# The first high part on VectorE, one more warm-up matmul, squares between the last pieces, the fourth unit ahead of the root's table, the last reciprocal ahead of a wait

## The chip, the cores and the metric

The kernel runs on one core of one Trainium2 chip. The metric is the device time of one execution in microseconds (us), the median of three runs. All input is in the chip's memory (HBM) at the start, and the output is written back there.

## What is computed

Two transformer blocks, one after the other, on a sequence of 256 tokens of width 1024, all in fp32. Cut to the steps:

```
# block 1
h = rmsnorm(x); proj = h @ w_in                  # 1024 -> 3*256 + 3*512 + 3*256
y = [stick_breaking_attention | chunked_relpos_attention | short_conv_mixer]
x = x + group_rmsnorm(y) @ w_out
x = x + (silu(n @ w_gate) * (n @ w_up)) @ w_down  # n = rmsnorm(x), width 2816
# block 2
h = rms_norm(x); proj = h @ w_in_2               # z_a, q, k, v, gate logits
y_a = chunked_spatial_gating(gelu(z_a)); y_b = dilated_mixture_attention(q, k, v)
x = x + (gate0 * (y_a @ w_branch_a) + gate1 * (y_b @ w_branch_b)) @ w_out_2
x = x + (gelu(conv3(a)) * val) @ w_down_2         # [a, val] = rms_norm(x) @ w_up_2
return rms_norm(x, final_norm_g)
```

rmsnorm(x, w) is x * rsqrt(mean(x*x) + 1e-6) * w. The change touches the first rmsnorm with the first units of the first product, and the last rms_norm.

## The kernel before

**Units.** All weights are laid out as one stream of units, each 128 partitions x 2048 columns of fp32 (1 MB). A ring of three slots holds them (RING = 3). SyncE's queue loads unit u into `raw[u % 3]` once the low part of unit u-3 is made (semaphore `unit_lo`). ScalarE casts the unit to fp32r, the high part (`split`, L525, writes `whi`, counts `unit_hi`), and VectorE subtracts it from the original, the low part (`split`, L978, writes `wlo`, counts `unit_lo`). TensorE multiplies high x high, low x high and high x low (helper `three`, L1594 to L1596; in other stages `tiles`, L1601 and L1602), which gives nearly fp32 accuracy at the speed of fp32r. The activations are split in the same way: `h_high` on ScalarE (L533) and `h_low` on VectorE (L989). Each engine runs its own instructions strictly in the order of the program; the order between engines comes from semaphores alone.

**The start.** The first three units come in ten pieces (`PIECES`): four of 512 columns for unit 0, four for unit 1, two of 1024 for unit 2. The activations x arrive transposed in five chunks. For each k of 8 ScalarE does `h_high(k)` and `split_piece(k)` (L530), VectorE `h_low(k)` and `split_piece(k)` (L984). TensorE first does WARM_UP = 8 matmuls of ones by ones (L1942), whose result nobody reads, and then `first_unit(0)` and `first_unit(1)`: for each k two matmuls of high x high (L1641), two with the low part of the weights (L1644), two with the low part of the activations (L1647). Behind the ten pieces ScalarE squares x in four steps (`square2`, L540), computes a small gain, and loads the table of the square root (`root_table`, L537). VectorE adds the squares (`fold(0)`, L995 to L998). Units 2 and 3 are `pair_unit`s: 24 matmuls for one half of the tokens, then 24 for the other half, and between the halves of unit 2 the sum of squares over the partitions (`stats(0)`, L1799).

**Behind it.** A hand-written order follows, the same on each engine: for n = 1, 2, ... a `split` of unit n + 2, then what the attention needs at that point. ScalarE at n = 2 issues the load of the bias table `relb` on its own queue (L677), takes the root (`root(0)`, L546), and scales q into `qkv_b` (L552); at n = 3 it casts unit 5 and squares q (`b_square(0)`, L630). VectorE sums these squares (`b_sums`, L1081) and normalises q (`b_norm`, L1087 and L1089). Between the halves of unit 4 TensorE transposes it (`turn_b(0)`, L1590).

**The end.** The last matmuls give the second half of the columns for tokens 128 to 255. VectorE adds them to x (L1576), multiplies by the gain (`final_gained`, L1549) and waits for this product (semaphore `dve_order`); ScalarE squares and takes the root (L958 to L960, L946); VectorE forms the reciprocal (L1563, in `final_scale`) and scales 640 columns (L1566), ScalarE the other 384 (L949), and six transfers in all write the output. `done` is a helper that lets the engine wait for its own instruction.

Of the kernel before, what the change touches and what calls it, by code (L numbers as in the profile page):

```python
# [33 lines left out]
HALF = UNIT // 2  # L34
UF = 256
WIDE = 512
WARM_UP = 8
RING = 3

D_SB, D_CH, D_CV = 256, 512, 256  # L40
# [190 lines left out]
def build(nc, A, out):  # L231
    with ExitStack() as ctx:
# [3 lines left out]
        def sem(name):  # L236
            return ctx.enter_context(nc.semaphore(name))
# [84 lines left out]
        bank = [psum[:, b, :] for b in range(8)]  # L322

        piece_loaded = [sem(f"piece_loaded{q}") for q in range(len(PIECES))]
        piece_hi, piece_lo = sem("piece_hi"), sem("piece_lo")
        unit_loaded = [sem(f"unit_loaded{s}") for s in range(RING)]
        unit_hi, unit_lo, unit_used = sem("unit_hi"), sem("unit_lo"), sem("unit_used")
        psum_full = [sem(f"psum_full{b}") for b in range(8)]
# [179 lines left out]
        def _(act):  # L508
# [18 lines left out]
            def split_piece(q):  # L527
                u, a, b = PIECES[q]
                act.wait_ge(unit_loaded[u % RING] if b == UNIT else piece_loaded[q], 16)
                act.copy(whi[u % RING][:, a:b], raw[u % RING][:, a:b]).then_inc(unit_hi if b == UNIT else piece_hi, 1)  # L530
# [8 lines left out]
            def square2(b):  # L539
                act.activation(sq[:, 2 * b:2 * b + 2, :], x[:, 2 * b:2 * b + 2, :], ACT.Square).then_inc(squares, 1)  # L540

            def root(n):

                b = STATS_BANK[n]
                full(act, b, ("stats", n))
                act.activation(rb[:], bank[b][:, 0:T], ACT.Sqrt, bias=EPS, scale=1.0 / D).then_inc(psum_free[b], 1)  # L546
# [41 lines left out]
            for k in range(KT):  # L588
                act.wait_ge(x_loaded[next(c for c, (a, b) in enumerate(X_CHUNKS) if a <= k < b)], 16)
                h_high("attn_norm", k)  # L590
                split_piece(k)
            split_piece(8)
            split_piece(9)
            for b in range(4):
                square2(b)
            act.wait_ge(cols_loaded, 16)
            act.activation(qgain[:], col("q_norm"), ACT.Copy, scale=HD ** -0.5).then_inc(act_order, 1)
            n_order[0] += 1
# [71 lines left out]
                return qkv_b[:, t, c:c + D_CH]  # L670

            for n in range(1, len(IN1)):
                if n == 1:
                    split(3)
                if n == 2:
                    split(4)
                    act.dma_start(relb[:], A["relb"]).then_inc(bias_loaded, 16)  # L677
                    root(0)
                    act.wait_ge(r_ready, 1)
                    evac_tokens(1, "qb", 0, qkv_cols("qb", 0))  # L680
                    evac_tokens(1, "qb", 1, qkv_cols("qb", 1))
                if n == 3:
                    split(5)
                    for t in range(TT):
                        freed(act, 6 + t, ("in1", "qb"))
                    b_square(0)
                    evac_tokens(1, "kb", 0, qkv_cols("kb", 0))
                    b_root(0)
                if n == 4:
                    evac_tokens(1, "kb", 1, qkv_cols("kb", 1))  # L690
                    for t in range(TT):
                        freed(act, t, ("in1", "kb"))
                    b_square(1)
                    split(6)
                    b_gains(0)
                    b_root(1)
                if n == 5:
                    split(7)
                    b_gains(1)
                    evac_tokens(1, "vb", 0, qkv_cols("vb", 0))  # L700
                if n == 6:
                    evac_tokens(1, "vb", 1, qkv_cols("vb", 1))
                    split(8)
                    b_exp(0)
                    b_exp(1)
                if n == 7:
                    b_evac_pt(0)
                    b_evac_pt(1)
                    split(9)
                    b_exp(2)  # L710
                    b_exp(3)
                if n == 8:
                    b_evac_pt(2)
                    b_evac_pt(3)
                    split(10)
                    b_exp(4)
                    b_exp(5)
                    for h in range(H_SB):
                        freed(act, ZA[h], ("za", h))
                    done(act.activation(E[:], Z[:], ACT.Abs))  # L720
                    done(act.activation(E[:], E[:], ACT.Exp, scale=-1.0))
                if n == 9:
                    full(act, 0, ("in1", "va"))
                    for t in range(TT):
                        ins = act.activation(v_a[:, t, :], bank[0][:, t * UF:(t + 1) * UF], ACT.Copy, scale=rcol[:, t:t + 1])
                    ins.then_inc(psum_free[0], 1)
                    b_evac_pt(4)
                    b_evac_pt(5)
                    split(11)
                    b_exp(6)  # L730
                    b_exp(7)
                    act.activation(E[:], E[:], ACT.Ln, bias=1.0).then_inc(z_soft, 1)
                if n == 10:
                    y_square(0)
                    b_evac_pt(6)
                    b_evac_pt(7)
                    split(U_OUT1)
                    y_rms(0)
                if n == 11:
                    split(U_OUT1 + 1)  # L740
                    freed(act, 0, ("in1", "xc"))
                    for f in range(2):
                        act.activation(cv[:, f, :], hc[:, f, 2:T + 2], ACT.Copy, scale=col("conv1", 3 * f + 2))\
                           .then_inc(cv_tap, 1)
                    y_square(1)
                    y_rms(1)
                    y_high(0)
                    for h in range(H_SB):
                        freed(act, AA[h], ("aa", h))
                    act.activation(E[:], Z[:], ACT.Exp).then_inc(z_w, 1)  # L750
# [213 lines left out]
        def _(dve):  # L964
# [15 lines left out]
            def split_piece(q):  # L980
                u, a, b = PIECES[q]
                s = u % RING
                dve.wait_ge(*((unit_hi, u + 1) if b == UNIT else (piece_hi, pieces_before(u) + 1 + a // (b - a))))
                dve.tensor_tensor(wlo[s][:, a:b], raw[s][:, a:b], whi[s][:, a:b], ALU.subtract)\  # L984
                   .then_inc(unit_lo if b == UNIT else piece_lo, 1)

# [2 lines left out]
                dve.scalar_tensor_tensor(lo[:, k, :], x[:, k, :], col(gain, k), hi[:, k, :], ALU.mult, ALU.subtract)\  # L989
                   .then_inc(h_lo, 1)  # L990

            def fold(n):

                dve.wait_ge(squares, 4 * n + 2)
                done(dve.tensor_tensor(sq[:, 0:2, :], sq[:, 0:2, :], sq[:, 2:4, :], ALU.add))  # L995
                dve.wait_ge(squares, 4 * n + 4)
                done(dve.tensor_tensor(sq[:, 4:6, :], sq[:, 4:6, :], sq[:, 6:8, :], ALU.add))
                ins = dve.tensor_tensor(sq[:, 0:2, :], sq[:, 0:2, :], sq[:, 4:6, :], ALU.add)  # L998
                if n == 0:
                    ins.then_inc(folded, 1)  # L1000
                else:
                    done(ins)
                    dve.tensor_tensor(sq[:, 0, :], sq[:, 0, :], sq[:, 1, :], ALU.add).then_inc(folded, 1)

            def gather(squares0, f):

# [61 lines left out]
                return dve.tensor_tensor(dst, dst, bc(rb[:], 1, 2), ALU.mult)  # L1068

            dve.wait_ge(consts, 1)  # L1070
            for k in range(KT):
                h_low("attn_norm", 0, k)
                split_piece(k)
            split_piece(8)
            split_piece(9)
            fold(0)

            def b_sums(j):

# [115 lines left out]
            def log_weights(h):  # L1195

                full(dve, AA[h], ("aa", h))
                dve.tensor_tensor(Z[:, h, :], Z[:, h, :], bank[AA[h]][:, 0:3 * P], ALU.add).then_inc(psum_free[AA[h]], 1)

            for n in range(1, len(IN1)):  # L1200
                if n == 1:
                    split(3)
                if n == 2:
                    rms_columns(0)
                    split(4)
# [73 lines left out]
                    h_low("ffn_norm", 1, 2 * b - 2)  # L1279
                    h_low("ffn_norm", 1, 2 * b - 1)  # L1280
            split(U_FF1 + 1)
            fold(1)

            def masks2():

# [265 lines left out]
            for u in range(U_DOWN2, N_UNITS):  # L1551
                split(u + 2)
                if u == U_DOWN2 + 6:
# [5 lines left out]
                    dve.wait_ge(final_sq, 2)  # L1559
                    dve.tensor_scalar(root_in, ss[:, 0:2], 1.0 / D, EPS, ALU.mult, ALU.add).then_inc(final_part, 1)  # L1560
            def final_scale(t):
                dve.wait_ge(final_root, t + 1)
                dve.reciprocal(root_out[:, t:t + 1], root_out[:, t:t + 1]).then_inc(final_r, 1)  # L1563
                dve.wait_ge(final_r, t + 1)
                for c in (slice(0, DVE_OUT // 2), slice(DVE_OUT // 2, DVE_OUT)):
                    dve.tensor_scalar(xg[:, t, c], xg[:, t, c], root_out[:, t:t + 1], None, ALU.mult).then_inc(out_ready, 1)  # L1566

            final_add(2)
            done(final_gained(2))
            final_scale(0)  # L1570
            final_add(3)
            for b, a, w in ((1, 0, CUT), (0, CUT, WIDE - CUT)):
# [7 lines left out]
               .then_inc(final_part, 1)  # L1580
            for b in range(2):
                freed(dve, b, ("rest2", b))
            done(final_gained(3))
            final_scale(1)


        @block.tensor
        def _(pe):
# [43 lines left out]
            def first_unit(u):  # L1632


                for kk in range(KT // 2):
                    k, w, last = u * KT // 2 + kk, slice(kk * WIDE, (kk + 1) * WIDE), kk == KT // 2 - 1
                    tokens = [slice(t * P, (t + 1) * P) for t in range(TT)]
                    pe.wait_ge(h_hi, k + 1)
                    pe.wait_ge(*((unit_hi, u + 1) if last else (piece_hi, pieces_before(u) + 1 + kk)))
                    for t, c in enumerate(tokens):  # L1640
                        pe.matmul(bank[6 + t][:], hh[:, k, c], whi[u][:, w], start=k == 0, stop=False)  # L1641
                    pe.wait_ge(*((unit_lo, u + 1) if last else (piece_lo, pieces_before(u) + 1 + kk)))
# [589 lines left out]
```

## Time and profile before

| | |
|---|---|
| median of 3 runs | 695.69 us (695.29 to 696.03) |
| the profiled execution | 695.99 us, of which the span is 694.0 us |
| TensorE matmul busy | 685.1 us, 99% of the span |
| VectorE busy | 498.4 us, 72% |
| ScalarE busy | 401.6 us, 58% |
| GpSimd busy | 9.4 us, 1% |
| read from HBM | 122.36 MB, 178 GB/s over the span |

The span is the time from the first to the last instruction of the core; the execution has 2.0 us more around it. Times in the rows are counted from the span's start. PE is TensorE, DVE VectorE, ACT ScalarE, SP SyncE; a letter q behind the engine means its queue. A row of the timeline gives start, duration, engine, line, operation, output<-inputs, shapes, and in brackets the idle time ahead of it with what ended it. Each instruction's record holds some pipeline time at its end, so that records of one engine overlap by 0.1 to 0.2 us: the distance from start to start is what an instruction costs in a row of them.

### The profile page before, as it was taken

Reading aid. Unit: us, or ns where it says so; the run is one execution under the profiler, and the core shown is the slowest. Engines: PE = TensorE matmul, PEld = TensorE weight load, DVE = VectorE, ACT = ScalarE, POOL = GpSimd, SP = SyncE. Lnnn points to the kernel's source line nnn. Section 1 sums busy time; section 2 is a strip of 40 time slices with the busy share of each in tenths; the row PEclk is TensorE's granted clock in tenths of the full one; section 3 lists DMA queues with packets and bytes.
Section 4 is the critical chain, followed back from the end, with each engine's and each line's share of the span. In section 5 each row is a group of like instructions: output and inputs, shape, how many; then the busy total and the mean of one; then the engine's idle time right before and its main releaser. Section 6 shows DMA issues by size and latency. Waiting matters only on the chain.

```text
span 694.0 us, 10061 instructions
## 1 busy us (share of the span) xinstructions
PE 685.1 (99%) x4118; PEld 602.7 (87%) x4118; DVE 498.4 (72%) x689; ACT 401.6 (58%) x504; POOL 9.4 (1%) x25
## 2 busy tenths in 40 slices
PE   8999999999999999999999999999999999999996
PEld 7889999888888888888878888899978888888885
DVE  5866677979986766666565477687779988886353
ACT  6875866755555554464457565564557666664342
POOL 1000000003000000000000000000000000000000
PEclk9999999999999999999999999999999999999999
DMA  8863225655565555545435346454555655554511
GB/s 322 316 232 135 90 93 183 220 183 193 179 219 187 194 182 182 187 178 193 171 124 180 122 138 226 160 181 146 182 211 182 203 184 189 200 196 175 190 60 61
DMA packets 19773, 124.05 MB, mean 179 GB/s; under 512 B 2320, under 2 KB 3472, under 8 KB 5520
## 3 DMA queue, kind: packets, MB, share of 16 engines
q1 hardware_dynamic: 18432, 120.07, 48.8%
q10 hardware_dynamic: 1296, 3.35, 1.4%
q8 instruction: 32, 0.52, 0.3%
q14 instruction: 13, 0.11, 0.0%
HBM read 122.36 MB, written 1.05 MB: 178 GB/s over the span
## 4 chain that ended last, share of the span: by engine, by line
PE 90%; DVE 4%; ACT 3%; issue 1%; DMA 1%; DVEq 0%; ACTq 0%
PE psum L1601 34%; PE psum L1602 18%; PE psum L1594 10%; PE psum L1596 10%; PE psum L1595 10%; PE psum L1590 2%; DVE wlo L978 2%; ACT whi L525 2%; PE psum L1641 1%; PE psum L2073 1%; PE psum L1647 1%; PE psum L1644 1%; DMA x<-in_xT 1%; PE psum L2121 0%; DVE gates L1496 0%
## 5 line engine op out<-in xcount | busy, mean ns | idle before, releaser
L978 DVE TENSOR_TENSOR wlo<-raw,whi 128x2048 fp32r<-128x2048 f32 x110 | 251.7, 2290 | 78.2 <-ACT whi L525 78.1
L525 ACT CAST whi<-raw 128x2048 fp32r<-128x2048 f32 x110 | 209.7, 1908 | 44.7 <-PE psum L1596 38.4
L1601 PE MATMUL psum<-hx,whi 128*128 128x512 f32 x528 | 183.6, 391 | 0.0
L1602 PE MATMUL psum<-hx,wlo 128*128 128x256 f32 x528 | 148.9, 282 | 0.0
L1601 PE MATMUL psum<-yx,whi 128*128 128x512 f32 x352 | 123.3, 393 | 1.1 <-DVE yx L989 1.0
L1601 PEld LDWEIGHTS psum<-hx,whi 128*128 128x128 f32 x528 | 99.1, 188 | 20.9 <-issue 0.2
L1602 PEld LDWEIGHTS psum<-hx,wlo 128*128 128x128 f32 x528 | 99.8, 189 | 0.0
L1602 PE MATMUL psum<-yx,wlo 128*128 128x256 f32 x352 | 99.2, 282 | 0.0
L1601 PEld LDWEIGHTS psum<-yx,whi 128*128 128x128 f32 x352 | 66.0, 188 | 15.7 <-DVE yx L989 2.1
L1602 PEld LDWEIGHTS psum<-yx,wlo 128*128 128x128 f32 x352 | 66.5, 189 | 0.0
L1601 PE MATMUL psum<-G,whi 128*128 128x512 f32 x176 | 61.8, 393 | 0.0
L1594 PE MATMUL psum<-whi,hx 128*128 128x512 f32 (+1 forms) x144 | 56.5, 392 | 0.0
L1595 PE MATMUL psum<-wlo,hx 128*128 128x512 f32 (+1 forms) x144 | 55.1, 383 | 0.0
L1596 PE MATMUL psum<-whi,hx 128*128 128x512 f32 (+1 forms) x144 | 55.1, 383 | 0.0
L1602 PE MATMUL psum<-G,wlo 128*128 128x256 f32 x176 | 49.8, 283 | 0.0
L1594 PE MATMUL psum<-hx,whi 128*128 128x256 f32 x144 | 41.0, 285 | 0.2 <-DVE hx L1509 0.2
L1595 PE MATMUL psum<-hx,whi 128*128 128x256 f32 x144 | 40.3, 280 | 0.0
L1596 PE MATMUL psum<-hx,wlo 128*128 128x256 f32 x144 | 40.2, 279 | 0.0
L1601 PEld LDWEIGHTS psum<-G,whi 128*128 128x128 f32 x176 | 33.1, 188 | 7.6
L807 ACT COPY us<-psum 128x512 f32<-128x512 f32 x22 | 12.9, 585 | 42.4 <-PE psum L1602 42.4
L800 ACT COPY side<-psum 128x512 f32<-128x512 f32 x22 | 12.9, 585 | 40.0 <-PE psum L1602 40.0
L1594 PE MATMUL psum<-yx,whi 128*128 128x256 f32 x128 | 36.0, 281 | 0.0
(271 smaller groups left out, 1107.0 us busy)
## 6 DMA issues: line engine op xcount, KB each, us to landing
raw<-in_stream SPq DMA_DIRECT2D x110, 1024.0 KB, 4.7
raw<-in_stream SPq DMA_DIRECT2D x8, 256.0 KB, 5.5
relb<-in_relb ACTq DMA_DIRECT2D x1, 1536.0 KB, 9.7
raw<-in_stream SPq DMA_DIRECT2D x2, 512.0 KB, 7.7
x<-in_xT SPq DMA_DIRECT2D x3, 256.0 KB, 5.5
out_t<-sq SPq DMA_DIRECT2D x4, 160.0 KB, 2.4
final_gain<-in_final_gain ACTq DMA_DIRECT2D x1, 512.0 KB, 3.5
bsp<-in_bsp ACTq DMA_DIRECT2D x1, 384.0 KB, 3.4
```

The costliest lines, as they stand in the source:

```text
L525: act.copy(whi[s][:], raw[s][:]).then_inc(unit_hi, 1)
L800: act.copy(side[:], psum[:, 0:2, T:2 * T]).then_inc(gate_side, 1)
L807: act.copy(us[:], psum[:, 2:4, T:2 * T]).then_inc(up_side, 1)
L978: dve.tensor_tensor(wlo[s][:], raw[s][:], whi[s][:], ALU.subtract).then_inc(unit_lo, 1)
L1590: return pe.transpose(out_, in_, ident[:])
L1594: pe.matmul(dst, stat[0], mov[0], start=first, stop=False, **kw)
L1595: pe.matmul(dst, stat[0], mov[1], start=False, stop=False, **kw)
L1596: return pe.matmul(dst, stat[1], mov[0], start=False, stop=last, **kw)
L1601: pe.matmul(bank[b][:], stat[0], mov, start=first, stop=False, skip_group_check=True)
L1602: return pe.matmul(bank[b][:, 0:T], stat[1], mov[:, 0, :], start=False, stop=last, skip_group_check=True)
L1641: pe.matmul(bank[6 + t][:], hh[:, k, c], whi[u][:, w], start=k == 0, stop=False)
L1644: pe.matmul(bank[6 + t][:], hh[:, k, c], wlo[u][:, w], start=False, stop=False)
```

## The change

Five edits:

1. VectorE, not ScalarE, makes the high part of piece 0, with a copy, and signals it on a new semaphore `first_hi`. VectorE and TensorE wait for it there; the counts on `piece_hi` are one lower in all other places.
2. WARM_UP is 9 instead of 8.
3. ScalarE squares x between the last pieces, and VectorE adds each pair of squares as it comes (`first_fold`, three adds in a chain) instead of `fold(0)`. The second block's fold keeps its form under the name `second_fold`.
4. ScalarE casts unit 3 right behind the squares, ahead of the small gain and the root's table; at n = 2 the load of the bias table and the root come ahead of the cast of unit 4. VectorE's order of its subtractions is as before.
5. In `final_scale` the product with the gain is issued, then the reciprocal waits only for the root, and the wait for the product stands behind the reciprocal.

```diff
-WARM_UP = 8
+WARM_UP = 9
@@ ScalarE
             for k in range(KT):
                 act.wait_ge(x_loaded[...], 16)
                 h_high("attn_norm", k)
-                split_piece(k)
+                if k:
+                    split_piece(k)
+            square2(0)
             split_piece(8)
+            square2(1)
             split_piece(9)
-            for b in range(4):
-                square2(b)
+            square2(2)
+            square2(3)
+            split(3)
             act.wait_ge(cols_loaded, 16)
@@
             for n in range(1, len(IN1)):
-                if n == 1:
-                    split(3)
                 if n == 2:
-                    split(4)
                     act.dma_start(relb[:], A["relb"]).then_inc(bias_loaded, 16)
                     root(0)
+                    split(4)
                     act.wait_ge(r_ready, 1)
@@ VectorE
             def split_piece(q):
                 u, a, b = PIECES[q]
                 s = u % RING
-                dve.wait_ge(*((unit_hi, u + 1) if b == UNIT else (piece_hi, pieces_before(u) + 1 + a // (b - a))))
+                if q == 0:
+                    dve.wait_ge(first_hi, 1)
+                elif b == UNIT:
+                    dve.wait_ge(unit_hi, u + 1)
+                else:
+                    dve.wait_ge(piece_hi, pieces_before(u) + a // (b - a))
@@
+            def first_fold(b):
+
+                dve.wait_ge(squares, b + 1)
+                if b > 1:
+                    dve.wait_ge(dve_order, n_order[0])
+                ins = dve.tensor_tensor(sq[:, 0:2, :], sq[:, 0:2, :], sq[:, 2 * b:2 * b + 2, :], ALU.add)
+                if b == 3:
+                    ins.then_inc(folded, 1)
+                else:
+                    ins.then_inc(dve_order, 1)
+                    n_order[0] += 1
@@
             dve.wait_ge(consts, 1)
-            for k in range(KT):
+
+            dve.wait_ge(piece_loaded[0], 16)
+            dve.tensor_copy(whi[0][:, 0:WIDE], raw[0][:, 0:WIDE]).then_inc(first_hi, 1)
+            split_piece(0)
+            h_low("attn_norm", 0, 0)
+            for k in range(1, KT):
                 h_low("attn_norm", 0, k)
                 split_piece(k)
             split_piece(8)
+            first_fold(1)
             split_piece(9)
-            fold(0)
+            first_fold(2)
+            first_fold(3)
@@
             def final_scale(t):
+                final_gained(2 + t).then_inc(dve_order, 1)
+                n_order[0] += 1
                 dve.wait_ge(final_root, t + 1)
                 dve.reciprocal(root_out[:, t:t + 1], root_out[:, t:t + 1]).then_inc(final_r, 1)
+                dve.wait_ge(dve_order, n_order[0])
                 dve.wait_ge(final_r, t + 1)
@@
-            done(final_gained(2))
             final_scale(0)
@@
-            done(final_gained(3))
             final_scale(1)
@@ TensorE
                     pe.wait_ge(h_hi, k + 1)
-                    pe.wait_ge(*((unit_hi, u + 1) if last else (piece_hi, pieces_before(u) + 1 + kk)))
+                    if k == 0:
+                        pe.wait_ge(first_hi, 1)
+                    else:
+                        pe.wait_ge(*((unit_hi, u + 1) if last else (piece_hi, pieces_before(u) + kk)))
```

## Rows read from the trace of the kernel before

**Rows 1.** Parts 1 and 2 of the page: busy time; TensorE's granted clock

```profile
PE 685.1 (99%) x4118; PEld 602.7 (87%) x4118; DVE 498.4 (72%) x689; ACT 401.6 (58%) x504; POOL 9.4 (1%) x25
...
PEclk9999999999999999999999999999999999999999
```

**Rows 2.** TensorE's waits, whole span: total us, times, longest

```profile
PE psum L1641 <- ACT whi L530: 0.7, 1, 0.7
```

**Rows 3.** Chain in order of time, first 12 us: start, duration

```profile
4.38 0.51 ACT hx L533
...
5.54 1.19 PE psum L1641 x2
...
8.44 0.84 PE psum L1641 x2
9.28 0.46 PE psum L1644 x2
```

**Rows 4.** Timelines of TensorE and VectorE, first 10 us

```profile
1.07 3.78 PE L1942 MATMUL psum<-ones 128*128 128x128 f32 x16 [1.07 <-POOL ones L469]
...
6.86 0.69 DVE L984 TENSOR_TENSOR wlo<-raw,whi 128x512 fp32r<-128x512 f32 x1 [0.34 <-ACT whi L530]
...
8.49 0.69 DVE L984 TENSOR_TENSOR wlo<-raw,whi 128x512 fp32r<-128x512 f32 x1 [0.55 <-ACT whi L530]
```

**Rows 5.** Transfers issued at 0.8 us: KB, us from issue to landing

```profile
raw<-in_stream SPq DMA_DIRECT2D x1, 256.0 KB, 3.4
```

**Rows 6.** Groups of VectorE by form: busy us, mean ns

```profile
L1290 DVE TENSOR_SCALAR mask<-mask 128x384 f32<-128x384 f32 x3 | 1.1, 362 | 0.1
```

**Rows 7.** Timelines of ScalarE, VectorE and TensorE, 15 to 24 us

```profile
15.70 1.06 ACT L530 CAST whi<-raw 128x1024 fp32r<-128x1024 f32 x1 [0.20 <-DMA raw<-in_stream]
...
20.37 3.91 ACT L525 CAST whi<-raw 128x2048 fp32r<-128x2048 f32 x2
...
19.68 0.69 DVE L998 TENSOR_TENSOR sq<-sq 128x512 f32<-128x512 f32 x1
...
18.44 0.40 PE L1594 MATMUL psum<-whi,hx 128*128 128x512 f32 x1
...
21.23 1.02 PE L1799 MATMUL psum<-sq,ones 128*128 128x256 f32 x4
```

**Rows 8.** Timelines of ScalarE, VectorE and TensorE, 26 to 34 us

```profile
26.61 1.91 ACT L525 CAST whi<-raw 128x2048 fp32r<-128x2048 f32 x1
28.41 1.06 ACT L630 ACTIVATE Z<-qkv_b 128x1024 f32<-128x1024 f32 x1
...
29.76 1.22 DVE L1081 TENSOR_REDUCE small<-Z 128x16 f32<-128x1024 f32 x1
...
31.55 1.22 DVE L1089 TENSOR_TENSOR qkv_b<-qkv_b,small 128x1024 f32<-128x1024 f32 x1
...
33.29 1.03 PE L1590 MATMUL psum<-ident,qkv_b 128*128 128x128 f32 x8
```

**Rows 9.** Transfers issued at 10.2, 18.0 and 22.4 us: KB, us to landing

```profile
raw<-in_stream SPq DMA_DIRECT2D x1, 1024.0 KB, 7.9
...
raw<-in_stream SPq DMA_DIRECT2D x1, 1024.0 KB, 8.3
...
relb<-in_relb ACTq DMA_DIRECT2D x1, 1536.0 KB, 9.7
```

**Rows 10.** Timelines of ScalarE and VectorE, 683 to 690 us

```profile
689.09 0.29 ACT L946 ACTIVATE small<-small 128x1 f32<-128x1 f32 x1
...
688.59 0.69 DVE L1549 TENSOR_TENSOR sq<-xt,final_gain 128x512 f32<-128x512 f32 x1
689.83 0.16 DVE L1563 RECIPROCAL small<-small 128x1 f32<-128x1 f32 x1 [0.55 <-ACT small L946]
...
683.62 0.29 ACT L946 ACTIVATE small<-small 128x1 f32<-128x1 f32 x1
...
684.02 0.17 DVE L1563 RECIPROCAL small<-small 128x1 f32<-128x1 f32 x1 [0.52 <-ACT small L946]
```

More of the change, by code:

```diff
@@ L324, in build @@
         piece_loaded = [sem(f"piece_loaded{q}") for q in range(len(PIECES))]
-        piece_hi, piece_lo = sem("piece_hi"), sem("piece_lo")
+        first_hi, piece_hi, piece_lo = sem("first_hi"), sem("piece_hi"), sem("piece_lo")
         unit_loaded = [sem(f"unit_loaded{s}") for s in range(RING)]
@@ L990, in h_low, with second_fold @@
                    .then_inc(h_lo, 1)
[L992 to L999, printed above, removed]
+            def first_fold(b):
[4 more added lines that the diff above has]
+                if b == 3:
                     ins.then_inc(folded, 1)
                 else:
-                    done(ins)
-                    dve.tensor_tensor(sq[:, 0, :], sq[:, 0, :], sq[:, 1, :], ALU.add).then_inc(folded, 1)
+                    ins.then_inc(dve_order, 1)
+                    n_order[0] += 1
+            def second_fold():
+                dve.wait_ge(squares, 6)
+                done(dve.tensor_tensor(sq[:, 0:2, :], sq[:, 0:2, :], sq[:, 2:4, :], ALU.add))
+                dve.wait_ge(squares, 8)
+                done(dve.tensor_tensor(sq[:, 4:6, :], sq[:, 4:6, :], sq[:, 6:8, :], ALU.add))
+                done(dve.tensor_tensor(sq[:, 0:2, :], sq[:, 0:2, :], sq[:, 4:6, :], ALU.add))
+                dve.tensor_tensor(sq[:, 0, :], sq[:, 0, :], sq[:, 1, :], ALU.add).then_inc(folded, 1)
             def gather(squares0, f):
@@ L1198, in log_weights @@
                 dve.tensor_tensor(Z[:, h, :], Z[:, h, :], bank[AA[h]][:, 0:3 * P], ALU.add).then_inc(psum_free[AA[h]], 1)
+            split(3)
             for n in range(1, len(IN1)):
-                if n == 1:
-                    split(3)
                 if n == 2:
@@ L1281, in _ @@
             split(U_FF1 + 1)
-            fold(1)
+            second_fold()
             def masks2():
```

## Prediction

> **What bounds the kernel now.** I read the page first: TensorE is busy for 685.1 of 694.0 us [rows 1]. Only what is left, some 9 us, can be had without taking work away. Next the view of TensorE's waits: 0.7 us lie before the first real matmul [rows 2], and the other waits are those of the start-up and some 1 us in the second block, far behind anything that is edited here. From the last matmul to the end of the span another 5.8 us pass, in which VectorE, ScalarE and the output transfers work. So a change at the front pays if TensorE's stream starts earlier or runs faster there, and if nothing behind it is then late; one at the tail pays in full.
>
> The chain of waits over the first 10 us shows two things [rows 3]. The stream is held by ScalarE, which does both halves of the first step in turn, the scaled activation at 4.38 and the first weight piece at 4.89; the first pair of matmuls starts at 5.54. And a pair of 512-column matmuls takes 0.84 us up to 9.28 and 0.46 us afterwards: TensorE runs at the lower of its two levels (1.2 GHz) until then, at 2.4 GHz from then on (the granted clock of the page reads 9 of 10 throughout, so the rows of the matmuls decide). Before the rise TensorE did eight warm-up matmuls from 1.07 to 4.85, sat idle for 0.69 us, and then worked without a gap [rows 2, 4].
>
> **The first high part on VectorE.** The first piece of weights lands 3.4 us after its issue at 0.81, at 4.2 [rows 5], before ScalarE begins its activation. VectorE has nothing to do until that activation ends at 4.89, since its first operation reads it. The copy of 128x512 has no row of its own: a one-source operation over 128x384 takes 0.36 us, the two-source one over 128x512 takes 0.69 [rows 4, 6]. So it ends between 4.7 and 4.95; I take 4.8, nearer the one-source row. ScalarE's activation ends at 4.89 [rows 3] and is the later of the two in most cases. Adding 0.14 from the end to the first matmul, as in the chain, the stream starts at 5.1, some 0.45 us earlier. At the low clock this is worth half, 0.23 us, if the clock still rises at 9.3. VectorE's low part is then due by 6.0 and is done by 5.6 at worst (4.95 and one 0.69): no new wait.
>
> The Trainium skill ("VectorE: DVE Perf Modes", mode 2x_2P) says that a copy from SBUF of 32-bit data can run at two elements a cycle, which two-source operations can't. The 0.36 against 0.69 us agrees; with 0.43 us the copy would be hidden behind ScalarE, with 0.69 it would decide, and the sum would differ by 0.03 us.
>
> **One more warm-up.** Eight took 3.78 us, 0.43 to 0.47 each [rows 4]. The ninth ends near 5.3 in the records; matmul records overlap by about 0.2 us, so its successor can start at 5.1. It costs nothing beyond the start found above and closes the idle 0.69 us. What that does to the clock no row shows. Lower bound: nothing, rise at 9.3. Upper bound: the rise comes at once, near the first real matmul. I take the early rise, because the only thing that TensorE lacked in its first 4.8 us against the stretch before 9.28 is that gap. TensorE can then run only as fast as the pieces come: the second piece's low part ends at 6.86+0.69=7.55, the third's at 8.49+0.69=9.18 [rows 4]; both hang on transfers, which the change leaves alone. With the third low part matmul pairs start at 9.3; from there two pairs (0.93 us) finish this step and five more steps of three pairs (1.40 us) follow: 9.3+0.93+7.0=17.25. Unit 2 begins at 18.44 now [rows 7]. Gain at this point: 1.2 us.
>
> The skill ("TensorE: Matmul & The Clock Gate", the HAM clock gate) says that sustained activity releases the clock, and also that the moment is not tied to the kernel's start and varies between runs. By the first half the early rise is likely; by the second no one profile can promise it, and the spread of 0.74 us among the three runs shown would in part be this.
>
> **Squares between the last pieces, and the fold in three adds.** ScalarE waits for both of the 1024-column pieces to land, 0.20 us for the second [rows 7], and half a us of square goes ahead of each, which these waits take up in part; the second piece's cast moves from 15.70 to 15.95. VectorE's second low part then ends at 18.5 instead of 18.0, just when a TensorE that is 1.2 us ahead wants it (17.25+1.4=18.65). The old fold ends at 20.37 and TensorE's sum of squares begins at 21.23 [rows 7]; 1.2 us earlier that would be 20.0, a 0.3 us wait. The new fold ends at about 19.9. So this edit is worth nothing alone and covers 0.3 us of the gain.
>
> **The fourth unit ahead of the root's table.** The table load goes behind the cast, which starts at 20.37 now [rows 7]; it can start at about 18.15, when the unit lands (10.2+7.9) [rows 9], 2.2 us earlier, and VectorE's low part with it: 18.15+1.9+2.3=22.4. TensorE takes that unit at about 21.23+0.9+2.8=24.9 now (the sum of squares, then twelve steps as from 18.44 to 21.23), at 23.7 if it is 1.2 ahead. Again cover, no gain by itself. The swap has more in it: the transfer of the bias table (1.5 MB, ScalarE's queue) is issued at about 21.6 instead of 22.4 [rows 9], the root comes before the fifth unit's cast, and SyncE's queue issues unit 5 at 18.55 instead of 18.05, as it waits for the second piece's low part, and unit 6 at 22.4, 2.2 us earlier.
>
> **What is late next.** Halfway through unit 4 TensorE transposes the normalised q (start 33.29). Its input is VectorE's multiply, which ends at 31.55+1.22=32.77 [rows 8]. With 0.13 us from there to TensorE, the slack is 0.38 us, less than the gain of 1.2. The chain behind it: unit 5, issued at 18.05, lands 8.3 us later at 26.35 [rows 9], ScalarE casts it at 26.61, then squares q at 28.41, VectorE sums at 29.76, and 3.01 us later the multiply is done [rows 8]. Now VectorE's long reciprocal also ends just before 29.76; after the change its work is some 1 us earlier, so the landing L of unit 5 decides: squares L+1.80, sums L+2.89, ready L+5.90, transposes L+6.03. With L as now 32.38, a gain of 0.91. L can move: unit 5's last bytes already share the engines with the bias table (9.7 us for 1.5 MB), which now starts 0.8 us earlier. I take L=26.5, gain 0.75; bounds 0.3 (L 0.6 later) and the full 1.2. Later transposes have more than 1 us of slack, and from unit 6 on everything is paced by TensorE.
>
> **The tail.** In the last chain ScalarE's root ends at 689.39, yet VectorE's reciprocal starts at 689.83, 0.44 us later, and its own multiply ended at 689.28; for the other tokens the root ended at 683.91 and the reciprocal began at 684.02 [rows 10]. The reciprocal is the instruction that carries the wait for VectorE's own multiply; the change moves this wait behind it. If the 0.4 us belong to the wait, ScalarE's part of the output gains 0.4 (VectorE's less, as its scaling now carries the wait); if not, one wait less is about 0.05. I take 0.25. A loss is excluded: the multiply is still issued before the root is there.
>
> **The sum.** Profiled execution 695.99 us (span 694.0 and 2.0 around it), less 0.75 and 0.25, is 695.0. The median of the runs shown is 0.3 us lower; the same 1.0 us from it gives 694.7.
>
> **The rivals.**
> 1. The gap was not what held the clock. The rise stays at 9.3, the front gives 0.23, nothing behind is late. 0.23+0.25=0.5 us: 695.2 (694.9 to 695.6). For it: the warm-ups are 128-column fp32 matmuls, not the later kind. Against it: nothing else differs before the rise. The same time comes out if the copy on VectorE is late.
> 2. Slower: the bias table, 0.8 us earlier, holds up unit 5's last bytes. Place: ScalarE's cast of unit 5, ahead of the square of q. It decides from L=27.25, where the transposes start as late as now. At L=28 TensorE loses 0.7 us, less 0.25 at the tail: 696.1. Against it: unit 5's bulk is in before the table starts.
> 3. Slower: the rise moves later, since it is not tied to the start. Each us later costs half a us, 3 us later 1.5, less the 0.5 of rival 1: 696.7.
> 4. More: unit 5 lands by 26.0, all 1.2 us pass, the tail gives 0.4, and the runs of before had the rise on average later than the profiled one (each us half a us): 693.8.
>
> **How the numbers follow.** Forecast 0.55 (694.1 to 695.3, from gains of 1.6 and 0.35), rival 1 0.25, rival 2 0.05, rival 3 0.05, rival 4 0.10. The range leaves out rivals 2 and 3 and the far end of 4: 693.9 to 695.6. A measurement of this kernel can tell some 0.2% (1.4 us) from no change, so faster means below 694.3: rival 4 and somewhat over a third of the forecast's case, 0.32. Slower means above 697.1: only rival 3 with a yet later rise, 0.05. The rest, 0.63, is the same.
>
> **What would show it.** Early rise: pairs of 0.46 us before 8 us and waits for the second and third piece. Cap at the transposes: TensorE waits up to 0.9 us for VectorE's multiply near 32.5. Rival 1: pairs of 0.84 us until about 9, no wait at all after the first. Rival 2: unit 5's cast after 27. Tail: reciprocal within 0.1 us of the root. The prediction is wrong if the transposes do not wait although the clock rose early, or if a step outside the first 35 us and the last 6 moves.

## The result and the profile after

The changed kernel takes 698.02 us (median of 12 runs, 695.82 to 700.37) against 695.35 (12 runs, 694.74 to 696.46): ratio 1.0031, 95% interval 1.0017 to 1.0046. It is slower by 0.3%, where 1.0 us of gain was forecast. The profiled execution took 696.45 us with a span of 694.7, against 694.0 before.

The start went as forecast. TensorE's timeline (start, duration; answers to [rows 4] and to the chain of [rows 3]):

```profile
1.07 4.21 PE L1967 MATMUL psum<-ones 128*128 128x128 f32 x18 [1.07 <-POOL ones L469]
4.99 0.97 PE L1666 MATMUL psum<-whi,hx 128*128 128x512 f32 x2
5.81 0.63 PE L1669 MATMUL psum<-wlo,hx 128*128 128x512 f32 x2
6.27 0.63 PE L1672 MATMUL psum<-whi,hx 128*128 128x512 f32 x2
```

No idle time stands ahead of the first real matmul any more, it starts at 4.99, and the pair that starts at 5.81 takes 0.46 us: the pace is that of the upper clock level, 3.5 us earlier than in the profile of before. (The granted clock reads 1.00 in both profiles all through the first 10 us, so, as in the prediction, it is the pace of the matmuls that decides. The pairs up to 9.8 us are further apart by up to 0.2 us, as TensorE now waits for the second and the third piece.) The copy on VectorE took 0.43 us and was over ahead of ScalarE's activation.

The loss is at the transposes of the normalised q. TensorE's waits, first 60 us, and its timeline around 32 us (answers to [rows 2] and [rows 8]):

```profile
PE psum L1612 <- DVE qkv_b L1111: 2.0, 1, 2.0
```

```profile
31.90 0.40 PE L1618 MATMUL psum<-whi,hx 128*128 128x512 f32 x1
34.30 1.09 PE L1612 MATMUL psum<-ident,qkv_b 128*128 128x128 f32 x8 [2.00 <-DVE qkv_b L1111]
```

TensorE comes to the transposes at 31.90+0.23=32.13, 1.16 us earlier than before, and can start them only at 34.30, 1.01 us later than before. ScalarE's timeline says where it comes from (answers to [rows 7] to [rows 9]; the last two are the views of the transfers issued at 17.9 on ScalarE's queue and at 18.2 on SyncE's, KB and us to landing):

```profile
17.84 1.91 ACT L525 CAST whi<-raw 128x2048 fp32r<-128x2048 f32 x1 [0.18 <-DMA raw<-in_stream]
17.85 0.33 ACTq L678 DMA_DIRECT2D relb<-in_relb  x1
19.66 0.20 ACT L601 ACTIVATE qgain<-cols 128x1 f32<-128x1 f32 x1
19.87 1.28 ACT L537 ACT_TABLE_LOAD   x1
...
28.27 1.91 ACT L525 CAST whi<-raw 128x2048 fp32r<-128x2048 f32 x1 [3.66 <-DMA raw<-in_stream]
```

```profile
relb<-in_relb ACTq DMA_DIRECT2D x1, 1536.0 KB, 9.2
...
raw<-in_stream SPq DMA_DIRECT2D x1, 1024.0 KB, 10.1
```

The load of the bias table stands in the program behind the cast of unit 3, the small gain and the root's table, which are over at 21.4. It was issued at 17.85, in the moment in which the cast of unit 3 began: here the computing ahead of a transfer did not hold its issue back, only the waits ahead of it did (here the last to be met is that for unit 3's landing). So it went out 0.3 us ahead of unit 5 (issued at 18.16) and 4.5 us earlier than before. The queues in 19.5 to 21.5 us (packets, MB, share of the 16 engines), changed kernel:

```profile
q10 hardware_dynamic: 59, 0.72, 89.4%
q1 hardware_dynamic: 5, 0.01, 1.1%
```

q10 is ScalarE's queue, q1 SyncE's: the bias table moves, unit 5 does not. Unit 5 lands at 28.3, ScalarE waits 3.66 us for it.

The tail gained. VectorE and ScalarE (answers to [rows 10]):

```profile
690.17 0.29 ACT L948 ACTIVATE small<-small 128x1 f32<-128x1 f32 x1
...
690.49 0.16 DVE L1586 RECIPROCAL small<-small 128x1 f32<-128x1 f32 x1
690.76 0.68 DVE L1590 TENSOR_SCALAR sq<-sq,small 128x320 f32<-128x320 f32 x2
```

The reciprocal starts 0.03 us behind the root's end instead of 0.44. From VectorE's last addition (689.29, before 688.21) to the span's end it is 5.4 us, before 5.8: 0.38 us less. The 1.08 us by which that addition is later and the 0.38 us back give the 0.7 us by which the profiled spans differ.

That leaves some 1.6 us between this profile and the median. Each run has its span and its mean granted TensorE clock. Five of the twelve, the profiled one among them, have spans of 694.1 to 694.9 us at 0.998 or 0.999; seven have 696.2 to 698.6 at 0.995 or 0.996. The 33 runs of before that stand beside the first experiments lie at 0.997 to 0.999. So in over half of the runs of the changed kernel the clock was low somewhere for longer; where, no profile of this kernel shows, as none was taken of such a run.

### The profile page after: what moved, and what is told of

Its sections match the earlier page's. It is cut to its first block, busy times and chain, and to the rows that moved or that the text cites. A ratio compares the mean times of both kernels' runs of the same rounds, so it can differ in the third digit from the quotient of the medians.

```text
span 694.7 us, 10066 instructions
## 1 busy us (share of the span) xinstructions
PE 684.7 (99%) x4120; PEld 601.5 (87%) x4120; DVE 498.9 (72%) x690; ACT 400.8 (58%) x503; POOL 9.3 (1%) x25
## 4 chain that ended last, share of the span: by engine, by line
PE 86%; DVE 5%; ACT 4%; DMA 2%; issue 2%; SPq 1%; DVEq 0%; ACTq 0%
PE psum L1623 34%; PE psum L1624 18%; PE psum L1616 10%; PE psum L1617 9%; PE psum L1618 9%; DMA raw<-in_stream 2%; PE psum L1612 2%; DVE wlo L980 2%; ACT whi L525 2%; PE psum L2098 1%; PE psum L2146 0%; DVE gates L1517 0%; SPq L428 0%; PE psum L2086 0%; DVE wlo L991 0%
```

## The experiments

The theories when they began. A: the bias table goes ahead of unit 5, TensorE idles 2 us at the transposes, and that idle time makes the clock fall in some of the runs. B: the clock falls because a TensorE that is fast from 5.6 us on has to wait for pieces in the first 10 us. C: the squares between the pieces and ScalarE's new order make the normalised q late. Each kernel has 10 to 12 runs, one has 7; each ratio is against the kernel before on the same chip.

**The bias table behind unit 5.** The changed kernel with

```diff
                 if n == 2:
-                    act.dma_start(relb[:], A["relb"]).then_inc(bias_loaded, 16)
                     root(0)
                     split(4)
...
                 if n == 3:
                     split(5)
+                    act.dma_start(relb[:], A["relb"]).then_inc(bias_loaded, 16)
```

> The changed kernel, with one line moved: the load of the bias table is issued behind ScalarE's cast of unit 5 (whose wait holds the issue back until unit 5 has landed) instead of ahead of the root. Theory A (the table's 1.5 MB, issued at 17.85, go ahead of unit 5; TensorE then waits 2.0 us for the normalised q, and in about half of the runs the clock falls because of that gap): unit 5 lands by 26.3, the transposes start by 32.4, TensorE's wait is under 0.5 us, all runs within 1 us of each other, clock 0.998 or more in all, median about 694.0 us. Theory B (the clock falls because TensorE, fast from 5.6 us on, waits for the second to third piece in the first 10 us): the spread of several us and clocks of 0.995 stay in about half of the runs, median 696 or more. Theory C (the squares between the pieces and the new order of ScalarE are late): unit 5 is cast early but the wait at the transposes stays near 2 us.

Measured: 694.17 us (693.83 to 694.51), ratio 0.9979 (0.9970 to 0.9988), the clock 0.997 to 0.999 in all eleven runs. ScalarE's and TensorE's timelines:

```profile
24.16 1.91 ACT L525 CAST whi<-raw 128x2048 fp32r<-128x2048 f32 x1
24.17 0.34 ACTq L685 DMA_DIRECT2D relb<-in_relb  x1
```

```profile
31.88 1.03 PE L1612 MATMUL psum<-ident,qkv_b 128*128 128x128 f32 x8
```

The queues in 19.5 to 21.5 us, to be set beside those above:

```profile
q1 hardware_dynamic: 96, 0.77, 95.7%
```

Unit 5 has landed when ScalarE wants it, the transposes start at 31.88 with no wait, 1.41 us earlier than before the change, and with the tail's 0.38 the span is 1.8 us shorter (692.2). One line turns the 0.3% loss into a 0.2% gain; this kernel (from here on the mended kernel) beats both. B and C are out: the early rise and the new order are all still in it, and the next kernel's profile has the waits for pieces in the first 10 us too.

**Behind unit 4.**

```diff
-                    act.dma_start(relb[:], A["relb"]).then_inc(bias_loaded, 16)
                     root(0)
                     split(4)
+                    act.dma_start(relb[:], A["relb"]).then_inc(bias_loaded, 16)
```

> The changed kernel, with the load of the bias table issued behind ScalarE's cast of unit 4, so at the landing of unit 4 (20.3 in the changed kernel's trace) instead of 17.85. Theory A: the table shares the engines with unit 5 for part of its way; unit 5 lands between 26 and 27.5, the transposes start between 32.1 and 33.6, median 694.3 to 695.5 us, a low clock only where the wait comes near 1.5 us, so rarely. Theory B: as slow and as spread as the changed kernel. Theory C: wait as in the changed kernel, 2 us.

Measured: 694.16 us (693.89 to 694.85), ratio 0.9981 (0.9972 to 0.9990). The table was issued at 20.80. Unit 4 had landed at 20.0 already; the last wait ahead of the issue is here the root's, for TensorE's sum of squares, whose last record ends at 20.69. Unit 5, issued at 17.95, landed 5.1 us later, earlier than theory A had it. Three us of delay for the table are as good as six: most of unit 5 has moved before the table's bytes begin.

**The bias table early, and nothing else.** The kernel before with

```diff
                 if n == 1:
                     split(3)
+                    act.dma_start(relb[:], A["relb"]).then_inc(bias_loaded, 16)
                 if n == 2:
                     split(4)
-                    act.dma_start(relb[:], A["relb"]).then_inc(bias_loaded, 16)
```

> The kernel before, with the load of the bias table issued behind the cast of unit 3 (about 20.4 us) instead of behind that of unit 4 (22.4). Nothing of the start is changed, so the clock rises as before and TensorE never waits in the first 10 us. Theory A: unit 5 lands some 1 to 2 us later, 27.3 to 28.3, the transposes start at 33.4 to 34.4 instead of 33.3, median 0.1 to 1.0 us above the kernel before, with single runs 1.5 us longer and at a clock of 0.995 if the wait is long enough. Theories B and C: as the kernel before, 695.4 us.

Measured: 696.58 us (695.11 to 698.68), ratio 1.0016 (1.0006 to 1.0026). The issue did not come at 20.4, as I had expected even then, but at 17.57, while ScalarE still had the root's table to load:

```profile
17.57 0.33 ACTq L675 DMA_DIRECT2D relb<-in_relb  x1
19.75 3.70 ACT L525 CAST whi<-raw 128x2048 fp32r<-128x2048 f32 x2
27.93 1.90 ACT L525 CAST whi<-raw 128x2048 fp32r<-128x2048 f32 x1 [1.91 <-DMA raw<-in_stream]
```

The transposes start at 33.96, after a wait of 1.3 us. The loss can be made from the kernel before by this one line. Unit 5 was issued 0.13 us ahead of the table here (17.44) and landed late all the same, at 27.9: from 20.0 to 22.5 us it moved 0.46 MB and the table 0.59. So the table does not have to overtake unit 5, to run beside it is enough. A run of 698.68 us has a clock of 0.996; the other ten have 0.997 to 0.999. The profile shows one thing that was not expected: the matmuls were at the upper pace from the first real one at 5.40 on, with eight warm-ups and 0.55 us of idle time. So the gap is not an absolute bar.

**A larger dose.** The changed kernel with 0.75 MB more on ScalarE's queue. The copy is not used; the output is the same.

```diff
                     act.dma_start(relb[:], A["relb"]).then_inc(bias_loaded, 16)
+                    act.dma_start(E[:], A["relb"][:, 0:H_SB, :]).then_inc(extra_loaded, 16)
...
+                    act.wait_ge(extra_loaded, 16)
                     done(act.activation(E[:], Z[:], ACT.Abs))
```

> The changed kernel with 0.75 MB more behind the bias table on the same queue (a second copy of its first half into a tile that is free then, and whose first use waits for it); the result is the same. A dose of the suspected cause: unit 5 lands some 2 us later, about 30.2 instead of 28.3, the transposes start near 36.2 and TensorE waits about 4 us ahead of them. If a gap in TensorE's work makes the clock fall, it falls in every run: the granted clock in the stretch behind the gap is below 1, matmuls there take 0.43 us, and the median is 2 us (stall) and a further 0.8 us or more (low clock in all runs rather than in half) above the changed kernel: 700.5 to 702 us. If the clock has nothing to do with the gap: 2 us above, 700.0, with the same share of low-clock runs.

Measured (7 runs): 698.32 us (696.26 to 699.27), ratio 1.0030 (1.0018 to 1.0043). The dose was smaller than meant: unit 5 was cast at 28.67 instead of 28.27, so part of the extra load can't have gone ahead of it. TensorE waited 2.9 us, not 4, and not every run has the low clock: four of seven, with 0.995 or 0.996, where the changed kernel has seven of twelve. The expectation failed on both points, and these runs do not show that a longer wait makes the low clock more frequent. What ties the clock to the wait is the profile, which caught one of the four. TensorE's timeline, and the stretches 35.0 to 35.5, 35.5 to 38.5 and 39 to 40 (after the busy times: granted clock, DMA share, GB/s):

```profile
34.70 1.51 PE L1614 MATMUL psum<-ident,qkv_b 128*128 128x128 f32 x8 [2.87 <-DVE qkv_b L1113]
35.87 0.78 PE L1618 MATMUL psum<-whi,hx 128*128 128x512 f32 x1
36.44 0.63 PE L1619 MATMUL psum<-wlo,hx 128*128 128x512 f32 x1
36.87 0.63 PE L1620 MATMUL psum<-whi,hx 128*128 128x512 f32 x1
...
38.58 0.43 PE L1618 MATMUL psum<-whi,hx 128*128 128x512 f32 x1
38.84 0.39 PE L1619 MATMUL psum<-wlo,hx 128*128 128x512 f32 x1
```

```profile
35.00:35.50 0.50, 0.50 (x6) 0.50 (x5) 0.50 (x1) 0.50 (x1) 0.00 (x0) 0.72 0.00 0
35.50:38.50 3.00, 3.00 (x10) 2.50 (x9) 2.72 (x3) 2.49 (x4) 0.00 (x0) 0.50 0.29 41
...
39.00:40.00 1.00, 1.00 (x6) 0.79 (x5) 1.00 (x2) 0.00 (x0) 0.00 (x0) 1.00 0.97 410
```

TensorE idles from 31.8 to 34.7, and half a us behind that, from about 35.2 on, the clock is granted by half (1.2 GHz): a 512-column matmul takes 0.43 us from start to start instead of 0.23, until about 38.6. Some 3.4 us at half speed cost 1.7 us, on top of the idle time ahead of them. That is most of the distance between the two groups of spans of the changed kernel (their medians are 694.4 and 696.5). And the low clock keeps to the kernels whose profiles have a wait at the transposes (this one, b_table_early, and the changed kernel, which was run twice): 14 of their 42 runs have a mean clock of 0.995 or 0.996. None of the 88 runs of the eight other kernels of this section has, and none of the 93 of the kernel before that stand beside them.

**The first high part and the ninth warm-up, on the kernel before.** Edits 1 and 2 alone.

> The kernel before with two of the edits alone: the first high part on VectorE, and nine warm-up matmuls. Theory A: the clock rises near 5.6 us, TensorE is about 1 us ahead until the transposes, where the normalised q is as late as before (32.8): a wait of about 0.7 us, transposes at 32.9, median 695.0 us, clock 0.998 or more in all runs. Theory B: runs of 697 us and more with a clock of 0.995 in about half of the cases. If the clock rises early by the idle gap alone, its profile shows pairs of 0.46 us from about 6 us on.

Measured: 694.88 us (694.45 to 695.17), ratio 0.9987 (0.9978 to 0.9995), the clock 0.997 to 0.999. TensorE comes to unit 3 some 0.3 us before its low part is made, and starts the transposes at 32.41 without a wait there, where 0.7 us of wait and 32.9 were expected. The median is as expected (695.0).

**The ninth warm-up alone.** `WARM_UP = 9` in the kernel before.

> The kernel before with nine warm-up matmuls instead of eight, and nothing else: the first real matmul comes at 5.54 as before, the gap ahead of it shrinks from 0.69 to about 0.25 us. Theory G (the length of the idle gap decides whether the clock rises early): early rise in nearly all runs, TensorE about 1 us ahead up to the transposes, median 694.9 to 695.2 us with a spread under 1 us. Theory H (nothing but the moment at which the chip looks decides; the profile of b_table_early shows a rise at 5.1 us with only eight warm-ups): as the kernel before, 695.6 us and a spread of 1.6 us.

Measured: 694.92 us (694.75 to 697.39), ratio 0.9994 (0.9986 to 1.0003). Nine of twelve runs lie between 694.75 and 695.5; two of 697 us have spans of 693.4 and 693.7 like the rest and lost their time outside the span, and they widen the interval. TensorE's timeline:

```profile
5.39 0.95 PE L1641 MATMUL psum<-whi,hx 128*128 128x512 f32 x2
6.18 0.62 PE L1644 MATMUL psum<-wlo,hx 128*128 128x512 f32 x2
6.64 0.63 PE L1647 MATMUL psum<-whi,hx 128*128 128x512 f32 x2
```

The first matmul comes 0.15 us earlier than in the profile of before (its input does), and the pairs are fast from about 6. Eleven of the twelve spans are 693.0 to 693.7 us; of the 31 of before on the same chip 12 are 693.8 or less and 19 lie at 694.0 to 694.6. This favours theory G, that the length of the gap decides how likely the early rise is; the interval of the ratio reaches over 1, so the times alone don't prove it.

**Eight warm-ups in the mended kernel.** `WARM_UP = 8` with the table behind unit 5.

> The mended kernel (bias table issued behind the cast of unit 5) with eight warm-up matmuls instead of nine. The gap between the warm-up and the first real matmul is then about 0.2 us (4.85 to 5.0). Theory G: a gap of 0.2 us is short enough in most runs, median 694.2 to 694.5, perhaps one or two runs near 695.5. Theory H: the same 694.2 as the mended kernel. If the ninth warm-up matters in itself, 694.8 and a spread above 1.2 us.

Measured: 694.05 us (693.76 to 694.50), ratio 0.9977 (0.9969 to 0.9986). Once VectorE makes the first high part, real work starts at 4.84 and closes the gap by itself; no gain of the ninth warm-up can then be measured.

**The tail alone.** Edit 5 in the kernel before.

> The kernel before with the last edit alone (the product with the gain issued, the reciprocal waiting only for the root, the wait for the product behind it). The changed kernel's trace shows the reciprocal 0.03 us behind the root instead of 0.44. If the 0.4 us belong to the wait: median 0.35 us below the kernel before, the last scalings 0.3 to 0.4 us earlier. If that gap is an accident of the instruction stream that moved with other edits: no difference.

Measured: 695.45 us (694.51 to 696.02) against 695.82, ratio 0.9993 (0.9984 to 1.0002). The 0.37 us are what was expected and no more than the noise. ScalarE's root, which ends at 689.84, and VectorE's reciprocal:

```profile
689.55 0.29 ACT L946 ACTIVATE small<-small 128x1 f32<-128x1 f32 x1
...
689.88 0.17 DVE L1565 RECIPROCAL small<-small 128x1 f32<-128x1 f32 x1
```

It starts 0.04 us behind the root's end. The profiles of b_warm9 and b_table_early, which have the old tail, show the old delay again: 0.46 us (root's end 688.49, reciprocal 688.95) and 0.47 us. But b_first_warm has the old tail too, and there the delay is 0.10 us:

```profile
688.19 0.29 ACT L947 ACTIVATE small<-small 128x1 f32<-128x1 f32 x1
...
688.58 0.16 DVE L1574 RECIPROCAL small<-small 128x1 f32<-128x1 f32 x1 [0.20 <-ACT small L947]
```

From VectorE's last addition to the span's end it is 5.5 us there, 5.4 in b_tail, 5.8 in the three others with the old tail. Those three have VectorE's program unchanged from end to end; b_first_warm has some instructions more at its start. So the old order does not cost the 0.4 us by itself. That the delay hangs on where the tail lies in VectorE's program, which this edit also moves, is the rival, named in the expectation, that stands untested; for the new order there is that none of its nine profiles shows more than 0.04 us.

**Once more the changed kernel,** on another chip, that of the next two.

> The changed kernel once more, on the chip of this call, as the yardstick for the next two. Theory A: two groups of runs again, one with a mean clock of 0.998 and a span near 694.5 us and one with 0.995 to 0.996 and a span near 696.5, median 696 to 698.5 us. If the first measurement was an accident of its chip, 695.7 us without a second group.

Measured: 696.36 us (695.68 to 699.21), ratio 1.0016 (1.0006 to 1.0027). TensorE waited 1.8 us at the transposes in its profile. The second group is there and smaller: two of twelve runs, 698.79 and 699.21 us at a clock of 0.995. What decides how many runs fall into it (the length of the wait, the chip, chance) is not shown; 698.02 or 696.36 is only a matter of whether these are more or fewer than half.

**The squares behind the pieces.** The mended kernel with

```diff
-            square2(0)
             split_piece(8)
-            square2(1)
             split_piece(9)
-            square2(2)
-            square2(3)
+            for b in range(4):
+                square2(b)
             split(3)
```

and VectorE's three adds behind its last piece.

> The mended kernel (bias table behind the cast of unit 5) without the edit on the squares: all four squares and the three adds stand behind the last two pieces, as before. The prediction called that edit cover for 0.3 us. With the three-add chain the fold then ends near 19.5 to 20.0 us and TensorE's sum of squares is due at 20.0, unit 3 is cast from 18.7 on: theory A expects a wait of at most 0.2 us at the sum of squares and the same median as the mended kernel, 694.2 us, within 0.3. If the squares between the pieces are what holds the gain, 694.7 or more.

Measured: 694.29 us (693.98 to 694.80), ratio 0.9980 (0.9972 to 0.9989), TensorE waits for none of the squares (its only wait on ScalarE there is 0.2 us at the first high part). The edit is worth nothing that can be measured.

**Edits 1, 2 and 5 on the kernel before.**

> The kernel before with the three edits that the runs so far show to be worth something: the first high part on VectorE, nine warm-ups, the reordered tail; squares, fold, unit 3 and the bias table as before. b_first_warm gave 694.9 us; the tail should take off another 0.35: 694.5 us, clock 0.997 or more in all runs, 0.3 us above the mended kernel, which would be what unit 3 ahead of the root's table is worth.

Measured: 694.78 us (694.42 to 695.76), ratio 0.9987 (0.9979 to 0.9996). The tail added nothing to edits 1 and 2 here (b_first_warm has the same ratio, 694.5 us were expected), which fits a b_first_warm without the long delay. The kernel with the squares behind the pieces is 0.5 us faster; between the two stand unit 3 ahead of the root's table, the later bias table and the fold in three adds. TensorE again waits 0.3 us for unit 3 here.

## Why the prediction was wrong

**The step that failed** is the sentence that the transfer of the bias table "is issued at about 21.6 instead of 22.4". I placed the issue behind all computing that stands ahead of it in ScalarE's program, the table load included. It goes out as soon as the last wait ahead of it is met, and with the swap that wait is unit 3's landing (17.85), no longer unit 4's (22.36). The statement in the description of the kernel, that each engine runs its own instructions strictly in the order of the program, holds for the computing, not for the issue of a transfer against it. The sign of that was in [rows 7] and [rows 9]: before, the issue stood in the program behind both of the casts that ran from 20.37 to 24.28, and it went out at 22.36, together with the start of the second:

```profile
22.36 1.92 ACT L525 CAST whi<-raw 128x2048 fp32r<-128x2048 f32 x1
22.36 0.33 ACTq L677 DMA_DIRECT2D relb<-in_relb  x1
```

The Trainium skill ("DMA: Bandwidth & Descriptors", Anatomy of one DMA) says that a semaphore wait happens on the issuing sequencer before the dispatch. The traces agree: the issue comes with the landing of unit 3 at 17.85 and 17.57, of unit 4 at 22.36, of unit 5 at 24.17, with the sum of squares at 20.80; and in the kernel with the squares behind the pieces at 24.02, when unit 5 had landed at 22.6 but TensorE's last matmul on unit 2, for which the cast of unit 5 also waits, ended at 23.92.

**The chain behind it was right.** The transposes were to start 6.03 us after unit 5 lands: 28.27+6.03=34.30, measured 34.30; in b_table_early 27.93+6.03=33.96, measured 33.96. That it fits to the last digit is in part luck: the sums start 0.08 us later than the prediction's term has it (31.24, not 28.27+2.89), and TensorE starts 0.05 us behind the multiply and not 0.13. L itself was the term that was wrong: 26.5 forecast, 28.3 measured, 24.2 with the table held back. Rival 2 named the place, the mechanism and the order of the price. It got 0.05, since I let the table start 0.8 us earlier and not 4.5.

**A term was missing.** Idle time at the transposes was priced at its own length. In part of the runs it costs more, as the clock falls behind it: 1.7 us in the one profile that shows it. Rival 3 had such a price, but at another place (a later rise).

**What was right.** The copy was hidden and TensorE starts at 4.99 (5.1 forecast). The early rise came, and most profiles fit the reason given: all nine of kernels with nine warm-ups show the rise between 4.1 and 6.8 us, and so does the one with eight in which VectorE's first high part closes the gap; with eight and the old start it came at 9.1 and 10.1 in two profiles and by 5.4 in one. In three of the nine, though, the pace rises during the warm-ups (about 4.1, 4.5 and 4.9 us), where no gap has been yet; so the runs favour the gap as what makes a late rise likely, and show that it is not all that decides. The gain up to the transposes was 1.16 us (1.2); the prediction's twelve matmuls for each half of the tokens in a pair unit are what the trace shows, not the 24 of the description of the kernel. That the squares and unit 3 only cover the gain held for the squares; unit 3 may be worth some of the 0.5 us between the mended kernel and the one with three edits, because TensorE waits 0.3 us for it otherwise; no run separates it from the later bias table. The tail gave 0.38 us in the profile (0.25 forecast, bound 0.4), but that the wait was the cause is not shown, as b_first_warm has the wait and a delay of only 0.10 us. With the table held back, the forecast's mechanism gives 1.5 us, more than the 1.0 forecast: unit 5 then lands near 24.2, so nothing caps the gain at the transposes.

## What to carry to other kernels

When a transfer's issue is moved in an engine's program, look not for the computing ahead of it but for the last wait ahead of it, and ask which transfer on another queue it will now overtake or run beside. Give a large load that is needed late (VectorE reads this one at 44.5 us) a wait that holds it behind the loads that are needed soon. Price an idle gap like those here (1.3 to 2.9 us) of a busy TensorE with the low clock behind it too, which came in 14 of 42 runs, and look at the clock of each run when a median moves and a profile doesn't. And before a delay is put down to one instruction's wait, look for a profile that has the wait and not the delay.

## What the runs showed of the hardware

- ScalarE's queue issued a transfer 3.5 us before the computing ahead of it was done (17.85, while the small gain and the root's table ran until 21.4).
- Two queues did not share the transfer engines evenly: in 19.5 to 21.5 us the bias table moved 0.72 MB and unit 5, issued 0.3 us later, 0.01 MB. In 22.0 to 24.5 us both moved about as much (0.57 and 0.46 MB), and so they did from 20.0 to 22.5 in b_table_early (0.59 and 0.46 MB), where unit 5 was issued 0.13 us ahead. Why the first stretch is so uneven is open.
- An idle time of 2.9 us in TensorE's work was followed by half the granted clock from about 35.2 to 38.6 us; by the mean clock of the runs the like befell seven and two runs of twelve with waits of 2.0 and 1.8 us in the profile, and one of eleven with 1.3 us.
- A reciprocal that carried the wait for VectorE's own earlier product started 0.44 to 0.47 us behind its other input in three profiles, although the product had ended 0.55 us before, and 0.10 us behind it in a fourth; with the wait on the next instruction it was 0.03 or 0.04 us in nine. What costs the 0.4 us is open.
